# Splitting the first condition into five pieces of one, two, two, two and one channel blocks in a hybrid decoder layer

## The reference

```python
ada = silu(c) @ w_ada + b_ada                    # 1024 -> 6 * 1024
sh_a, sc_a, g_a, sh_f, sc_f, g_f = split(ada, 6)
h = rmsnorm(x, norm_mix_w) * (1.0 + sc_a) + sh_a
x = x + g_a * token_mixer(h, w_in, ...)          # h @ w_in, two gated linear attentions, @ w_out
h = rmsnorm(x, norm_ffn_w) * (1.0 + sc_f) + sh_f
x = x + g_f * conv_ffn(h, w_up, ..., w_down)
out = rmsnorm(x, final_norm_w)
```

## Time and profile before

| what | value |
|---|---|
| median of 3 runs | 903.09 us |
| lowest and highest | 902.99 and 903.15 us |
| the profiled execution | 903.03 us |
| its span in the trace | 901.3 us |
| mean granted TensorE clock | 0.999 |
| instructions | 13464 |

### The profile page before, as it was taken

One profiled execution on the slowest core, in us unless ns is written; L12 is line 12 of the kernel. 1 busy time (PEld: TensorE's weight loads), 2 busy tenths in 40 slices (PEclk: granted clock), 3 DMA queues, 4 the chain that ended last, 5 costly groups with the idle time before them and its releaser, 6 DMA issues.

```text
span 901.3 us, 13464 instructions
## 1 busy us (share of the span) xinstructions
PE 886.0 (98%) x4798; PEld 732.7 (81%) x4798; DVE 498.0 (55%) x678; ACT 452.9 (50%) x694; POOL 182.4 (20%) x179
## 2 busy tenths in 40 slices
PE   7999999999999999999999989999999999999997
PEld 6778888888888888888887868888888888888885
DVE  4558755656556565555765466645544444733327
ACT  5486665556555565555666444433333333522224
POOL 2121342213422134221343000211111111100000
PEclk9999999999999999999999999999999999999999
DMA  9958344362343613437207921533333332323202
GB/s 337 373 159 233 103 129 142 113 190 56 110 141 106 196 53 110 137 107 199 67 27 218 133 70 48 161 96 93 93 93 94 101 108 95 117 94 103 84 0 94
DMA packets 145732, 112.16 MB, mean 124 GB/s; under 512 B 3559, under 2 KB 137025, under 8 KB 145440
## 3 DMA queue, kind: packets, MB, share of 16 engines
q1 hardware_dynamic: 145104, 110.84, 41.9%
q0 software_dynamic: 592, 0.86, 0.3%
HBM read 107.49 MB, written 4.20 MB: 124 GB/s over the span
## 4 chain that ended last, share of the span: by engine, by line
PE 91%; issue 3%; DVE 2%; ACT 2%; POOL 1%; DMA 1%; POOLq 0%; DVEq 0%; ACTq 0%
PE ps L1392 26%; PE ps L1394 26%; PE ps L1393 26%; PE ps L1473 2%; PE ps L1557 1%; PE ps L1646 1%; PE ps L1647 1%; PE ps L1650 1%; PE ps L1559 1%; PE ps L1539 1%; PE ps L1417 1%; PE ps L1409 1%; PE ps L1523 1%; DVE w_lo L927 0%; PE ps L1526 0%
## 5 line engine op out<-in xcount | busy, mean ns | idle before, releaser
L927 DVE TENSOR_TENSOR w_lo<-raw,w_hi 128x1024 fp32r<-128x1024 f32 x142 | 184.2, 1308 | 120.7 <-ACT w_hi L599 120.1
L1392 PE MATMUL ps<-h_hi,w_hi 128*128 128x512 f32 x560 | 219.1, 391 | 0.0
L1394 PE MATMUL ps<-h_hi,w_lo 128*128 128x512 f32 x560 | 217.9, 389 | 0.0
L1393 PE MATMUL ps<-h_lo,w_hi 128*128 128x512 f32 x560 | 217.9, 389 | 0.0
L1392 PE MATMUL ps<-w_hi,h_hi 128*128 128x512 f32 x520 | 205.8, 396 | 0.2 <-DVE w_lo L927 0.2
L1394 PE MATMUL ps<-w_hi,h_lo 128*128 128x512 f32 x520 | 202.5, 389 | 0.0
L1393 PE MATMUL ps<-w_lo,h_hi 128*128 128x512 f32 x520 | 202.4, 389 | 0.0
L599 ACT ACTIVATE w_hi<-raw 128x1024 fp32r<-128x1024 f32 x142 | 147.0, 1052 | 75.3 <-PE ps L1394 48.8
L1392 PEld LDWEIGHTS ps<-h_hi,w_hi 128*128 128x128 f32 x560 | 105.1, 188 | 22.2 <-issue 0.5
L1393 PEld LDWEIGHTS ps<-h_lo,w_hi 128*128 128x128 f32 x560 | 105.1, 188 | 22.1 <-issue 0.5
L1394 PEld LDWEIGHTS ps<-h_hi,w_lo 128*128 128x128 f32 x560 | 105.1, 188 | 21.8
(11 more groups left out here) (231 smaller groups left out, 967.2 us busy)
## 6 DMA issues: line engine op xcount, KB each, us to landing
raw<-in_w_in_dram SPq DMA_DIRECT2D x68, 512.0 KB, 4.4
raw<-in_w_up_dram SPq DMA_DIRECT2D x44, 512.0 KB, 3.8
ada_w<-in_w_ada_dram SPq DMA_DIRECT2D x32, 512.0 KB, 4.2
raw<-in_w_down_dram SPq DMA_DIRECT2D x22, 512.0 KB, 3.3
ada_w<-in_w_ada_dram SPq DMA_DIRECT2D x8, 1024.0 KB, 10.3
raw<-in_w_out_dram SPq DMA_DIRECT2D x8, 512.0 KB, 7.7
x_tok<-in_x_dram SPq DMA_DIRECT2D x4, 512.0 KB, 8.6
w_first<-in_w_in_dram SPq DMA_DIRECT2D x8, 256.0 KB, 8.5
```

Source lines behind the costliest of these rows:

```text
L927: dve.tensor_tensor(w_lo[:, slot(u)].rearrange("p k c -> p (k c)"), raw[:, raw_slot(u)].rearrange("p k c -> p (k c)"), w_hi[:, slot(u)].re ...
L1392: pe.matmul(dst, a_hi, b_hi, start=start and i == 0, stop=False)
L1393: pe.matmul(dst, a_hi, b_lo, start=False, stop=False)
L1394: last = pe.matmul(dst, a_lo, b_hi, start=False, stop=stop and i == n - 1)
```

## The change

The first condition is worked out in five pieces, of blocks 0, 1-2, 3-4, 5-6 and 7. The loads, the splits of w_first (first_hi, first_lo), ada0_finish and the loop on DVE follow the table PIECE. In a piece of one block the sums use the four column groups for two contraction blocks and two vectors, so 16 instructions stand where a piece of two blocks has 32, and a matmul with a small matrix `pick` (two columns that each add two of the groups) stands in place of the transpose. The sums of piece 1 go between the first four and the second four matmuls of k = 0, its turn ahead of the last four. The sums of pieces 2, 3 and 4 stand behind k = 1, 3 and 4, their turns in k = 2, 4 and 5. On ACT the takes and first_hi of pieces 1 to 4 stand behind h_full of k = 0, 2, 4 and 6. keep_busy at the start goes from 12 to 7. Two semaphores are added so that hi_made and lo_made still count four for the first units.

```diff
-PIECES = KT // 2
-SUMS_AFTER = {0: 1, 2: 2, 4: 3}
-TURN_IN = {1: 1, 3: 2, 5: 3}
+PIECE = ((0, 1), (1, 2), (3, 2), (5, 2), (7, 1))
+PIECES = len(PIECE)
+PIECE_OF = (0, 1, 1, 2, 2, 3, 3, 4)
+SUMS_AFTER = {1: 2, 3: 3, 4: 4}
+TURN_IN = {2: 2, 4: 3, 5: 4}
...
             def ada0_loads(i):
+                k0, nb = PIECE[i]
                 for a in range(2):
-                    c0 = a * D + 2 * i * P
-                    sp.dma_start(ada_w0[:, i % 2, :, a], wada_v[:, :, c0:c0 + 2 * P]).then_inc(ada0_in[i], 16)
+                    c0 = a * D + k0 * P
+                    sp.dma_start(ada_w0[:, i % 2, :, a, 0:nb * P], wada_v[:, :, c0:c0 + nb * P]).then_inc(ada0_in[i], 16)
...
-                if k in (1, 3, 5):
+                if k in (0, 2, 4, 6):
                     ada0_take(k // 2 + 1)
                     first_hi(k // 2 + 1)
...
+            dve.wait_ge(const_made, 3)
+            dve.tensor_tensor(pick, ident[:, 0:2 * 32:32], ident[:, 2 * 32:P:32], ALU.add).then_inc(pick_made, 1)
...
             def ada0_sums(i):
 
+                nb = PIECE[i][1]
                 pe.wait_ge(ada0_in[i], 32)
                 pe.wait_ge(ada0_row_made, i)
-                for k in range(KT):
+                for k in range(0, KT, 3 - nb):
                     for j in range(4):
...
+                if PIECE[i][1] == 1:
+                    pe.wait_ge(pick_made, 1)
+                    pe.matmul(ps[:, bank, 0:2], ada_row[:], pick, start=True, stop=True).then_inc(ada0_turned, 1)
+                else:
+                    pe.transpose(ps[:, bank, 0:P], ada_row[:], ident[:]).then_inc(ada0_turned, 1)
...
-            keep_busy(12)
+            keep_busy(7)
...
                     values(t, k, h_hi, w_hi)
...
+                if k == 0:
+                    ada0_sums(1)
...
                 for t in range(TT):
                     values(t, k, h_hi, w_lo)
+                if k == 0:
+                    ada0_turn(1)
```

More of the change, by code:

```diff
@@ L170, in build @@
         qscale = cols[:, 58:59]
+        pick = cols[:, 42:44]
         frs = cols[:, 54:58]
@@ L621, in first_hi @@
             def first_hi(i):
+                k0, nb = PIECE[i]
                 act.wait_ge(w_first_in[i], 32)
-                act.activation(w_hi[:, 0:4, 2 * i:2 * i + 2].rearrange("p u k c -> p k u c"),
-                               w_first[:, 2 * i:2 * i + 2], ACT.Copy).then_inc(hi_made, 1)
+                act.activation(w_hi[:, 0:4, k0:k0 + nb].rearrange("p u k c -> p k u c"),
+                               w_first[:, k0:k0 + nb], ACT.Copy).then_inc(hi_made if i < 4 else late_hi_made, 1)
             def roots(a, b, count):
@@ L941, in ada0_finish @@
             def ada0_finish(i):
-                k0 = 2 * i
+                k0, nb = PIECE[i]
                 def part(ap):
-                    return ap.rearrange("p (a b) -> p a b", b=KT)[:, :, k0:k0 + 2]
+                    return ap.rearrange("p (a b) -> p a b", b=KT)[:, :, k0:k0 + nb]
                 dve.wait_ge(ada0_turned, i + 1)
-                dve.tensor_tensor(part(ada[:, 0:16]),
-                                  ps[:, 3 if i else 1, 0:P].rearrange("p (a b c) -> p a b c", b=2, c=32)[:, :, :, 0],
-                                  part(vecs[:, V_BADA:V_BADA + 16]), ALU.add).then_inc(ada0_made, 1)
+                bank = 3 if i else 1
+                if nb == 1:
+                    sums = ps[:, bank, 0:2].unsqueeze(2)
+                else:
+                    sums = ps[:, bank, 0:P].rearrange("p (a b c) -> p a b c", b=2, c=32)[:, :, :, 0]
+                dve.tensor_tensor(part(ada[:, 0:16]), sums, part(vecs[:, V_BADA:V_BADA + 16]), ALU.add
+                                  ).then_inc(ada0_made, 1)
                 dve.wait_ge(ada0_made, 2 * i + 1)
-                dve.scalar_tensor_tensor(out=a_mix[:, k0:k0 + 2], in0=ada[:, 8 + k0:10 + k0], scalar=1.0,
-                                         in1=vecs[:, V_NMIX + k0:V_NMIX + k0 + 2],
+                dve.scalar_tensor_tensor(out=a_mix[:, k0:k0 + nb], in0=ada[:, 8 + k0:8 + k0 + nb], scalar=1.0,
+                                         in1=vecs[:, V_NMIX + k0:V_NMIX + k0 + nb],
                                          op0=ALU.add, op1=ALU.mult).then_inc(ada0_made, 1)
@@ L971, in first_lo @@
             def first_lo(i):
[L973 to L976, removed]
+                k0, nb = PIECE[i]
+                if i < 4:
+                    dve.wait_ge(hi_made, i + 1)
+                else:
+                    dve.wait_ge(late_hi_made, 1)
+                part = w_hi[:, 0:4, k0:k0 + nb].rearrange("p u k c -> p k u c")
+                dve.tensor_tensor(w_lo[:, 0:4, k0:k0 + nb].rearrange("p u k c -> p k u c"),
+                                  w_first[:, k0:k0 + nb], part.bitcast(F32), ALU.subtract
+                                  ).then_inc(lo_made if i < 4 else late_lo_made, 1)
             def turn_taken(t, half):
@@ L1014, in _ @@
             dve.wait_ge(xT_made_dve, X_DVE)
-            for i in range(PIECES):
+            for i, (k0, nb) in enumerate(PIECE):
                 if i:
@@ L1411, in ada0_sums @@
             def ada0_sums(i):
+                nb = PIECE[i][1]
                 pe.wait_ge(ada0_in[i], 32)
                 pe.wait_ge(ada0_row_made, i)
-                for k in range(KT):
+                for k in range(0, KT, 3 - nb):
                     for j in range(4):
-                        last = pe.matmul(ps[32 * j:32 * j + 32, 7, 0:P], c_rep[:, k],
-                                         ada_w0[:, i % 2, k, j // 2, (j % 2) * P:(j % 2 + 1) * P],
-                                         start=k == 0, stop=k == KT - 1)
+                        k_in, a, b = (k + j // 2, j % 2, 0) if nb == 1 else (k, j // 2, j % 2)
+                        last = pe.matmul(ps[32 * j:32 * j + 32, 7, 0:P], c_rep[:, k_in],
+                                         ada_w0[:, i % 2, k_in, a, b * P:(b + 1) * P],
+                                         start=k == 0, stop=k + 3 - nb == KT)
                 last.then_inc(ada0_summed, 1)
@@ L1480, in _ @@
             for k in range(KT):
-                pe.wait_ge(hi_made, k // 2 + 1)
+                piece = PIECE_OF[k]
+                if piece < 4:
+                    pe.wait_ge(hi_made, piece + 1)
+                else:
+                    pe.wait_ge(late_hi_made, 1)
                 pe.wait_ge(h_hi_made, k + 1)
@@ L1488, in _ @@
                     values(t, k, h_hi, w_hi)
-                pe.wait_ge(lo_made, k // 2 + 1)
+                if k == 0:
+                    ada0_sums(1)
+                if piece < 4:
+                    pe.wait_ge(lo_made, piece + 1)
+                else:
+                    pe.wait_ge(late_lo_made, 1)
                 for t in range(TT):
                     values(t, k, h_hi, w_lo)
+                if k == 0:
+                    ada0_turn(1)
                 if k == KT - 1:
```

20 lines of the change are left out of this document (13 added, 7 removed).

## The result

| | before | after |
|---|---|---|
| median of 9 runs each | 904.55 us | 906.11 us |
| lowest and highest | 902.99 and 904.76 us | 905.96 and 908.28 us |
| profiled execution | 903.03 us | 906.27 us |
| its span | 901.3 us | 904.5 us |

The ratio of the two kernels' runs is 1.0029, with a 95% interval of 1.0021 to 1.0038: slower, by 1.9 to 3.4 us. The two medians alone give 1.0017, since the median of before lies in the upper of two groups; either way all nine runs of after are longer than all nine of before. The three runs that the prediction knew and the trace that it is argued from belong to the first. The trace of after is 3.2 us longer than that of before; the medians are 1.6 us apart.

What follows compares the result with a forecast made beforehand. PE, busy 98% of the span, was taken as the bound. Start - 2.0, bubbles + 1.45 and + 1.6, longer list + 0.95 and + 0.1 gave + 2.1 us: 905.2 against the median 903.09, range 903.8 to 907.0.

Steps and rivals of the forecast that it cites:

- Two bubbles: PE waits in the loop: 1.45 us ahead of k = 1 and 1.6 us at the turn of piece 4.
- the wait for piece 1: In k = 0, PE waits 0.4 us ahead of the second sums, for piece 1 landing at 19.1 to 19.2.
- half a sum more: Sums in the loop go from three full ones to three full and one half: + 0.95 us.
- a turn more: Turns in the loop go from three to four, delaying PE's matmuls around one: + 0.1 us.
- The second bubble: In k = 5, PE waits 1.6 us at the turn of piece 4, whose take on ACT stands behind h_full(6).
- the term of 2.4 us: Ahead of the loop, halving the first piece brings x and the first product 2.4 us earlier, between 2.1 and 3.0.
- The start gains 2.0 us on PE's list: Up to the second sums: 2.4 us earlier less 0.4 us of waiting for piece 1 gives 2.0 us.
- The late clock: Second rival: fewer identity matmuls leave PE at its lower clock level at the start; + 1.8 us more, 907.0; chance 0.1.
- The rival with the larger gain of the start: First rival: 512-byte rows cost nothing, piece 1 lands at 18.6, the start gains 2.5 us; + 1.6, 904.7; chance 0.14.
- The third rival: In the loop, piece 2 or 4 lands behind its sums; 906.2 for 1 us over the slack; chance 0.12.

Runs made afterwards that it cites:

- second trace of after: The changed kernel, unchanged, run once more for another trace; the run took 906.65 us.
- the run without that wait: The changed kernel with ACT's take of piece 4 moved from behind h_full of k = 6 to behind h_full of k = 5; 904.65 us.
- run 24: Not a label: in "in one run 24 records", 24 counts records; that run is the changed kernel, unchanged, traced once more; 906.65 us.

## Why the prediction came out as it did

It forecast a loss of 2.1 us, 905.2 in a range of 903.8 to 907.0, with 0.63 on slower by over 0.2%. The median is 906.11, and the direction is right. Between the two traces, 903.03 to 906.27, the loss is 3.24 us, so the forecast is short by 1.1. Between the medians of nine runs it is 1.56 us, less than forecast, because of the second group of before, which the prediction didn't know. Measured that way it comes out nearer than its sum deserves.

- The mechanism of the loop was right. Two bubbles (1.45 and 1.6), the wait for piece 1 (0.4), half a sum more (0.95) and a turn more (0.1) make + 4.5; the loop is 4.51 us longer. That the sum agrees to 0.01 is luck, since its parts differ. The second bubble is 1.4 us, from 42.14 + 0.57 (two matmuls, as between 32.74 and 33.31 of the earlier trace rows) to 44.12. The first is about 1.4, from 23.18 + 0.95 to 25.50. The wait for piece 1 is only about 0.15: from the first product to the second sums it is 1.26 us, and 1.09 in the second trace of after, where nothing was waited for. Half a sum is 1.0, and the turns cost 0.26 more, most of it at the turn with pick, which has 0.25 us of PE (44.12 to 44.37) after its wait and 0.14 in the run without that wait. Some 0.3 us is left, spread over small gaps where the matmuls are cut apart. Taking the second bubble away gave back 1.46 us.
- The start was mis-sized, and this is the step that failed: the term of 2.4 us for the bytes of piece 0, which was laid on all later landings, on x ("so x lands earlier by the time of 1 MB") and then on piece 1 ("It now lands earlier by 2.4 (piece 0) and 0.7 [...], at 19.1 to 19.2"). Piece 0 did land 2.4 us earlier (9.35 to 6.95). The tiles of x did not: the first landed at 9.3 in place of 10.7, 1.4 us earlier, and the last at 13.3 in place of 14.4, 1.1 us earlier. Piece 1 landed at 20.2, 2.1 us earlier and not 3.1, and the first product moved by 1.24 and not 2.4. The issue of the first tile with its us to landing, before and after, and the chain of after, which names the transfer of piece 1 with start and length:

```profile
2.36 1.34 SPq L407 DMA_DIRECT2D x_tok<-in_x_dram  x1
x_tok<-in_x_dram SPq DMA_DIRECT2D x1, 512.0 KB, 8.3
...
2.36 1.25 SPq L414 DMA_DIRECT2D x_tok<-in_x_dram  x1
x_tok<-in_x_dram SPq DMA_DIRECT2D x1, 512.0 KB, 6.9
```

```profile
6.88 13.31 DMA ada_w<-in_w_ada_dram
20.19 0.04 issue
20.23 1.95 PE ps L1440 x64
```

- From the second sums on the rest came as forecast: k = 6 was to follow them by 45.6 - 19.15 = 26.45 us and did by 26.51. The miss of 1.1 us is that these sums start at 20.23 and not at 19.15. Two things meet there, and both were late: the landing at 20.19, and PE, which from 18.97 would have come to the sums at about 20.06 (the 1.09 us of above). With piece 1 at 19.15 this trace would have won only some 0.15 us, an estimate from these rows, since the late tiles and the late clock held PE; with 12 identity matmuls PE is ready at about 19.0 and the landing, at 19.5, is what remains. Both hang on the term of 2.4 us.
- The error was to shift all later landings by the time of the bytes removed, at a steady rate. Neither half of that held. The bytes: when the first tile was in, the queue had moved 3.07 MB before (until 10.67) and 2.36 MB after (until 9.3), so 0.71 MB less and not 1.05; more of the later transfers had gone ahead of the tile's last bytes. The first w_first transfer, issued behind all tiles, even landed at 12.5, ahead of the last tile at 13.3; before it was the other way round (15.3 and 14.4). The rate: by 8 us the queue of after was 0.10 MB behind that of before, by 20 us 0.33 MB (6.29 and 6.62), which at 385 GB/s is 0.9 us. A part of that arose between 12 and 14. What the queue moved between 12 and 14, and between 14 and 20 us, first before and then after:

```profile
12.00:14.00 2.00, 1.00 1.03 410
14.00:20.00 6.00, 1.00 1.06 364
```

```profile
12.00:14.00 2.00, 1.00 1.01 289
14.00:20.00 6.00, 1.00 1.09 382
```

  After shows a dip to 289 GB/s where x gives way to w_first and piece 1; against 385 GB/s that is 0.5 us, and with 1 KB rows in piece 0 the landing was no earlier. Before has lower rates a little later, so part of the dip is common to both. Why the engines fall behind just there, and why later transfers get ahead, is not settled. The landing of piece 1 spread over 1.1 us from run to run and variant: 19.5 with 12 identity matmuls, 20.2 in after, 20.6 with rows of 1 KB.
- "The start gains 2.0 us on PE's list, and this number goes by the landing of piece 1 alone" was right in its second half by only 0.15 us for the first trace (the gain itself was 1.1 us and not 2.0) and not for the second, where the late clock made PE the later one. The late clock, given 0.1, did come in every trace of this layout with 7 identity matmuls: 32 records of sums take 1.93 us or more. What it was priced at is not what it did. At the first product it cost at most 1.03 us in one pair of traces and 0.15 in the other, most of it hid behind piece 1, and putting the 12 back gained nothing in either median. The rival that counted on a late clock through all x_turns (907.0) comes near the second trace, where three of the four tiles were turned late and the run took 906.65.
- The rival with the larger gain of the start fell: it needed piece 1 at 18.6. The Trainium skill's 512 bytes for line rate ("DMA: Bandwidth & Descriptors", Specifications) would bear this rival out, but it doesn't agree with the 0.7 us by which the same bytes landed sooner in rows of 1 KB. That difference didn't reach piece 1.
- The third rival, a later piece late, didn't come in the changed kernel: behind k = 1 the periods are those of before, 28.43 to 36.17, 7.74 us between sums, as between 30.86 and 38.59. It named pieces 2 and 4, though, and the one with little slack was piece 3, landing at 35.2 for sums at 36.17. Once the bubbles were shortened it cost 0.41 us in one trace.
- What the prediction couldn't see from three runs is the second group of runs of the kernel before. Against it the changed kernel loses less, 1.6 us between medians and not 3.2.

## What to carry to other kernels

Price a reordering by two lists at once: where the producer's step stands on its engine and where the consumer's stands on its own. The take behind k = 6 and its turn inside k = 5 cost 1.4 us, all visible beforehand, and moving that one take gave it back. When the load that gates a loop is made smaller, ask which load gates next and from what chain it hangs: here piece 1's landing plus sums, take, turn and 2.4 us of chain put k = 1 at 25.5, where it was 25.0 before any piece was split, so the earlier first product was worth nothing. When a wait on PE is taken away, ask the same of the loads behind it. And where loads saturate the queue, don't shift a later landing by the bytes removed without a margin of a microsecond, and look at the nearest landing first: the tiles already showed the miss here.

## What the runs showed of the hardware that was not expected

- The same transfer of the same kernel lands at times almost 2 us apart: the last token tile at 14.4 us in one run (SP's issue at 4.72 plus 9.7) and 16.3 in another (4.64 plus 11.7), though the queue moved 401 to 406 GB/s from 6 to 12 us in both; from 12 to 14 us it moved 410 and 374. In two more traces with the same loads it landed at 14.6 and 15.75. In the pair of traces 1.07 us at the first product goes with 1.12 us of time, and the two groups are 1.5 us apart. What makes the tile late isn't known.
- After 3.35 us of identity matmuls and 1.1 us of idling PE's records still come at the lower level's distance (0.06 us for a record of sums, where 0.03 is the upper), and in one run 24 records of token tiles took 4.89 us, where 2.93 us was their time in the first trace of the kernel before; with 4.80 us of filling the sums run at the upper level at 7.26.
